# One weight slot per direction of a recurrence, and two projection tiles between its last links

## The reference, cut to what matters

```python
p = jnp.einsum('bsd,de->bse', h, w_in)
u, q, k, v, zr, gl = jnp.split(p, IN_SPLITS, axis=-1)
y_a = multiscale_pool(u, pool_w, pool_scale)
y_b = diff_attention(q, k, v, ...)
y_c = rwkv7_bidir(zr, ...)
```

```python
def step(state, inp):
    r_t, w_t, k_t, v_t, kk_t, a_t = inp
    sa = jnp.einsum('bhij,bhj->bhi', state, -kk_t)
    state = (state * w_t[:, :, None, :] + sa[..., None] * (kk_t * a_t)[:, :, None, :]
             + v_t[..., None] * k_t[:, :, None, :])
    return state, jnp.einsum('bhij,bhj->bhi', state, r_t)
...
y = direction(0, False) + direction(1, True)
mu = jnp.mean(y, axis=-1, keepdims=True)
var = jnp.mean(jnp.square(y - mu), axis=-1, keepdims=True)
y = ((y - mu) * lax.rsqrt(var + GN_EPS)).reshape(b, s, RW_WIDTH) * gn_g + gn_b
```

## Time and profile before

| | |
|---|---|
| median of 3 runs | 3981.09 us (3978.69 to 3983.14) |
| span of the profiled execution, first to last instruction | 3976.1 us |
| PE, busy | 3783.7 us (95%) |
| DVE, ACT, POOL, busy | 1684.3, 1439.1, 1388.7 us |
| transfers | 356.65 MB, 90 GB/s |
| mean granted TensorE clock | 0.984 |

### The profile page before, as it was taken

The page is one execution under the profiler, slowest core; times in us unless marked ns, Lnnn a source line. Parts: engine busy times, 40 slices in busy tenths (PEclk is TensorE's granted clock), DMA queues, the critical chain, the costliest instruction groups (busy, mean ns, idle before and its releaser), DMA issues.

```text
span 3976.1 us, 67100 instructions
## 1 busy us (share of the span) xinstructions
PE 3783.7 (95%) x28976; PEld 3059.2 (77%) x28976; DVE 1684.3 (42%) x2714; ACT 1439.1 (36%) x2442; POOL 1388.7 (35%) x581
## 2 busy tenths in 40 slices
PE   8888999999999889999999989999999999999999
PEld 7777778788887776688888776777888777787887
DVE  5554541577145554603682257414111376332112
ACT  3354252232323442523223243634222436424222
POOL 4001324434442002244444354133444443244443
PEclk9999999999999999999999999999999999999999
DMA  3001222276220002122473221112222221122222
GB/s 143 2 4 45 82 75 85 85 251 222 93 87 33 4 4 91 66 85 106 161 269 123 93 85 64 43 64 101 92 99 88 103 85 39 51 103 84 86 101 90
DMA packets 37150, 356.65 MB, mean 90 GB/s; under 512 B 4224, under 2 KB 4352, under 8 KB 17920
## 3 DMA queue, kind: packets, MB, share of 16 engines
q1 hardware_dynamic: 19584, 278.93, 18.9%
q10 hardware_dynamic: 17280, 73.48, 5.2%
HBM read 350.29 MB, written 2.10 MB: 89 GB/s over the span
## 4 chain that ended last, share of the span: by engine, by line
PE 84%; DVE 8%; ACT 3%; issue 2%; POOL 1%; DMA 1%; DVEq 0%; SPq 0%; PEldq 0%; ACTq 0%; PEld 0%; POOLq 0%
PE banks L757 23%; PE banks L759 23%; PE banks L758 22%; PE banks L1110 10%; PE banks L2151 3%; ACT arena L1471 1%; ACT arena L2304 1%; PE banks L2233 1%; POOL ring_r L855 1%; DMA ring<-stream 1%; DVE arena L1949 1%; DVE arena L2628 1%; PE banks L1217 0%; DVE arena L2627 0%; DVE arena L1843 0%
## 5 line engine op out<-in xcount | busy, mean ns | idle before, releaser
L855 POOL TENSOR_TENSOR ring_r<-ring,hi_ring 128x1024 fp32r<-128x1024 f32 x490 | 1202.4, 2458 | 2252.0 <-ACT hi_ring L846 2250.9
L757 PE MATMUL banks<-xT_r,ring_r 128*128 128x512 f32 (+1 forms) x2480 | 955.6, 385 | 25.8 <-issue 14.1
L759 PE MATMUL banks<-xT_r,hi_ring 128*128 128x512 f32 x2096 | 829.2, 396 | 0.0
L758 PE MATMUL banks<-x_lo_r,hi_ring 128*128 128x512 f32 x2096 | 825.4, 394 | 0.0
L846 ACT ACTIVATE hi_ring<-ring 128x1024 fp32r<-128x1024 f32 x490 | 511.3, 1047 | 734.0 <-DMA ring<-stream 289.2
L757 PEld LDWEIGHTS banks<-xT_r,ring_r 128*128 128x128 f32 x2480 | 472.5, 191 | 124.5 <-issue 26.7
L759 PEld LDWEIGHTS banks<-xT_r,hi_ring 128*128 128x128 f32 x2096 | 396.1, 189 | 94.1
L758 PEld LDWEIGHTS banks<-x_lo_r,hi_ring 128*128 128x128 f32 x2096 | 398.2, 190 | 90.3 <-issue 3.3
L1110 PE MATMUL banks<-arena 64*64 64x64 f32 (+4 forms) x7456 | 350.0, 246 | 53.0 <-DVE arena L1843 23.8
L1471 ACT ACTIVATE arena<-banks 128x512 f32<-128x512 f32 x366 | 214.7, 595 | 413.8 <-PE banks L759 255.2
L757 PE MATMUL banks<-hi_ring,pairs 128*128 128x512 f32 x864 | 341.8, 396 | 4.0 <-POOL ring_r L855 4.0
(11 more groups left out here) (263 smaller groups left out, 5504.1 us busy)
## 6 DMA issues: line engine op xcount, KB each, us to landing
ring<-stream SPq DMA_DIRECT2D x132, 2048.0 KB, 7.7
arena<-ada ACTq DMA_DIRECT2D x96, 512.0 KB, 4.9
arena<-ln_rows ACTq DMA_DIRECT2D x5, 1024.0 KB, 7.7
arena<-edge ACTq DMA_DIRECT2D x4, 1024.0 KB, 5.1
arena<-edge ACTq DMA_DIRECT2D x2, 1792.0 KB, 8.3
arena<-pack ACTq DMA_DIRECT2D x2, 1485.0 KB, 6.6
arena<-pack ACTq DMA_DIRECT2D x2, 1200.5 KB, 5.5
x<-x_in SPq DMA_DIRECT2D x4, 512.0 KB, 7.4
```

The lines of the kernel that those rows point to most:

```text
L757: first = nc.tensor.matmul(out_, left[1], right[0], start=start, stop=False)
L758: low = nc.tensor.matmul(out_, left[0], right[1], start=False, stop=False)
L759: return first, low, nc.tensor.matmul(out_, left[0], right[0], start=False, stop=stop)
L855: nc.gpsimd.tensor_tensor(feed.raw(n, ring_r), feed.raw(n), feed.hi(n).bitcast(F32), ALU.subtract).then_inc(split_lo, 1)
```

## The change

The matrices of a direction move into one slot each: direction 0 into the slot of unit 4, direction 1 into the slot of unit 5 (3072 columns of `GM`, 1024 of `WU`). Each slot is given back alone: behind link 6 of group 6 the one of direction 0, behind link 6 of group 7 the other (`slot_back`, a drain and one count each). `u`'s weights thus load while group 7 is computed. Its first tile is made in four parts of 6 products behind links 2, 3, 4 and 5 of group 7, the second in four, behind link 6, behind `y_out` (two) and behind the last mean. The pieces of `u` are split at `oo` of group 7, its links 1 and 5, and at the third part of the second tile; the third waits until group 6 is through, because its place in `hi_ring` holds that group's matrices. Three means go behind `mq`, `oo` and link 0 of group 7, the fourth behind `y_out`. The sums of squares go behind `u` 2, `gn_turn` behind `u` 3, and one `gn_out` behind each tile of `q`. Banks change with it.

```diff
--- before.py
+++ after.py
@@ -83,6 +83,8 @@
 EPS2 = 1e-6
 INDEX_SCALE = (64 ** -0.5) * (8 ** -0.5)
 UNITS1 = 35
+U_UNIT = 4
+U_PARTS = 2
 UNITS2 = 31
 X_LO = 27504
 W_HI = X_LO + 4096
@@ -173,8 +175,8 @@
                 ([] if last else [("inv_x", g, n, banks_x)]) + [("inv_t", g, n, banks_t)]]
     out += [[("wu", g, (b0, b1))], [("mq", g, (b0, b1))], [("oo", g, ())]]
     out += [[("link", g, i, (4 + i % 2,) if i < NC - 1 else ())] for i in range(NC)]
-    if g == GROUPS - 1:
-        out[-2].append(("ring_back", ()))
+    if g >= GROUPS - 2:
+        out[-2].append(("slot_back", d, ()))
     if d:
         out[-1].append(("y_out", j, (7,)))
     return out
@@ -248,22 +250,29 @@
         for n, beat in enumerate(beats_of(g)):
             if g or n >= AHEAD_BEATS:
                 late.setdefault(OFFSET * g + n - AHEAD_BEATS, []).append(beat)
+    end = GROUPS - 1
+    tail = {("mq", end): [("gn_mean", 0)], ("oo", end): [("gn_mean", 1)], ("link", end, 0): [("gn_mean", 2)],
+            ("link", end, 2): [("u_part", 0, 0)], ("link", end, 3): [("u_part", 0, 1)], ("link", end, 4): [("u_part", 0, 2)],
+            ("link", end, 5): [("u", 0)], ("link", end, 6): [("u_part", 1, 0)], ("y_out", PAIRS - 1): [("u_part", 1, 1)]}
+    tail_banks = {"gn_mean": (0, 1), "u_part": (), "u": (2, 3)}
     for n in sorted(late):
         for beat in late[n]:
             for part in beat:
                 add(*part[:-1], banks=part[-1])
-    for j in range(PAIRS):
-        add("gn_mean", j, banks=(j % 2,))
-    add("gn", banks=(0,))
-    behind = {("u", 1): [("gn_turn",)], ("u", 2): [("gn_out", 0)], ("u", 3): [("gn_out", 1)], ("q", 1): [("gn_out", 2)],
-              ("q", 3): [("gn_out", 3)],
+                for more_, i, *rest in tail.get(part[:-1], []):
+                    add(more_, i, *rest, banks=tail_banks[more_][i % 2:][:1])
+    add("u_part", 1, 2)
+    add("gn_mean", PAIRS - 1, banks=(1,))
+    add("u", 1, banks=(3,))
+    behind = {("u", 2): [("gn",)], ("u", 3): [("gn_turn",)], ("q", 0): [("gn_out", 0)], ("q", 1): [("gn_out", 1)],
+              ("q", 2): [("gn_out", 2)], ("q", 3): [("gn_out", 3)],
               ("k", 0): [("pool_mix", 0)], ("k", 1): [("pool_mix", 1), ("pool_lo", 0)],
               ("k", 2): [("pool_mix", 2), ("pool_lo", 1)], ("k", 3): [("pool_mix", 3), ("pool_lo", 2)]}
     for name in "uqk":
-        for i in range(4):
-            add(name, i, banks=(4 + i % 2,))
+        for i in range(U_PARTS if name == "u" else 0, 4):
+            add(name, i, banks=(2 + i % 2 if name == "u" else 4 + i % 2,))
             for late_, *at_ in behind.get((name, i), []):
-                add(late_, *at_, banks={"gn_turn": (1,), "gn_out": (0, 1, 2), "pool_mix": (sum(at_) % 2,)}.get(late_, ()))
+                add(late_, *at_, banks={"gn": (6,), "gn_turn": (6,), "gn_out": (0, 1, 6), "pool_mix": (sum(at_) % 2,)}.get(late_, ()))
     add("pool_lo", 3)
     add("v_open", banks=(2, 3, 4, 5))
     for i in range(4):
@@ -343,8 +352,9 @@
             add("next", ((2, 3, None, 7), (2, 4, 6, 9))[layer][tt])
     if layer == 0:
         add("turn", 1, 3, banks=(0, 4))
-    out = with_splits(out, first_pieces(), {ZT: ("u", 0), UP_PIECE + HEAD: ("turn", 0, 3)},
-                      {UP_PIECE + i: (("out_tile", 2), ("out_tile", 3))[i // 2] for i in range(HEAD)}, HEAD)
+    out = with_splits(out, first_pieces(), {ZT + 4: ("u", 2), UP_PIECE + HEAD: ("turn", 0, 3)},
+                      {**{UP_PIECE + i: (("out_tile", 2), ("out_tile", 3))[i // 2] for i in range(HEAD)},
+                       ZT: ("oo", end), ZT + 1: ("link", end, 1), ZT + 2: ("link", end, 5), ZT + 3: ("u_part", 1, 2)}, HEAD)
     return number(out)
 
 
@@ -436,7 +446,9 @@
 
 def first_pieces():
 
-    out = tile_pieces("z", 0, ZT) + tile_pieces("u", 4, 4) + tile_pieces("q", 5, 4) + tile_pieces("k", 6, 4) + row_pieces("v", 7)
+    out = tile_pieces("z", 0, ZT) + tile_pieces("u", U_UNIT, 4) + tile_pieces("q", 5, 4) + tile_pieces("k", 6, 4) + row_pieces("v", 7)
+    for i in range(U_PARTS):
+        out[ZT + i] = (("u_part", i, 0),) + out[ZT + i][1:]
     for n in range(3):
         out += tile_pieces("gate", 8 + 3 * n, DT, (n,)) + branch_pieces(n, 10 + 3 * n)
     out += row_pieces("out", 17, (0,)) + tile_row_pieces(18)
@@ -1009,8 +1021,14 @@
     BB = [arena[:, a_:a_ + 1024].rearrange("p (a t) -> p a t", a=2) for a_ in (17768, 18792)]
     X, XT, T1 = [[arena[:, a_ + 512 * d:a_ + 512 * d + 512].rearrange("p (b t) -> p b t", b=8) for d in range(2)]
                  for a_ in (19816, 20840, 21864)]
-    GM = [ring[:, 3072 * d:3072 * d + 3072].rearrange("p (q e b a t) -> p q e b a t", q=4, e=2, b=2, a=3) for d in range(2)]
-    WU = [ring[:, 6144 + 1024 * d:7168 + 1024 * d].rearrange("p (q e a t) -> p q e a t", q=4, e=2, a=2) for d in range(2)]
+    def in_slot(layer, d):
+
+        return UNIT * ((layer * UNITS1 + U_UNIT + d) % RING)
+
+    GM_of = [[ring[:, a_:a_ + 3072].rearrange("p (q e b a t) -> p q e b a t", q=4, e=2, b=2, a=3)
+              for a_ in (in_slot(layer, 0), in_slot(layer, 1))] for layer in range(L)]
+    WU_of = [[ring[:, a_ + 3072:a_ + UNIT].rearrange("p (q e a t) -> p q e a t", q=4, e=2, a=2)
+              for a_ in (in_slot(layer, 0), in_slot(layer, 1))] for layer in range(L)]
     AR0 = [arena[:, a_:a_ + 1024].rearrange("p (q e a t) -> p q e a t", q=4, e=2, a=2) for a_ in (22888, W_HI)]
     QM = [chunks(arena[:, a_:a_ + 1024], 2) for a_ in (W_HI + 1024, W_HI + 2048)]
     state = arena[:, 26984:27240].rearrange("p (d i k) -> p d i k", d=2, i=2)
@@ -1104,6 +1122,7 @@
 
     def first_tensor(pe, k_, layer, uses):
         feed = feed1[layer]
+        GM, WU = GM_of[layer], WU_of[layer]
         seen = {}
 
         def mm(out_, lhsT, rhs, start, stop):
@@ -1119,7 +1138,7 @@
                 return False
             seen[n] = True
             feed.wait_loaded(pe, n)
-            return n > 0 and n not in (3, 4)
+            return n > 0 and n not in (U_UNIT - 1, U_UNIT)
 
         def step(name, *args):
             banks, use = uses[(name,) + tuple(args)]
@@ -1134,6 +1153,14 @@
                     for turned in (0, 4):
                         pe.wait_ge(bank_free[turned], 2 - TT)
                 feed_product(pe, feed, feed.at["z", args[0]], bank[b][:, 0:S // 2], begin, x_pair, tokens=slice(0, S // 2))
+            elif name == "u_part" or name == "u" and args[0] < U_PARTS:
+                (b,), (n,) = uses[("u", args[0])]
+                part = args[1] if name == "u_part" else 3
+                if part == 0:
+                    take(b, n)
+                ins = feed_product(pe, feed, feed.at["u_part", args[0], 0], bank[b][:, :], begin, x_pair, part=part)
+                if part == 3:
+                    ins.then_inc(bank_full[b], 1)
             elif name in ("z", "u", "q", "k"):
                 i, b = args[0], banks[0]
                 head = name == "z" and i < HEAD
@@ -1327,9 +1354,9 @@
                              False, d == 1 and i == NC - 1)
                 if i == NC - 1:
                     ins.then_inc(*((bank_full[y_bank], 1) if d else (halves_done, 1)))
-            elif name == "ring_back":
-
-                pe.drain().then_inc(weights_used, RING)
+            elif name == "slot_back":
+
+                pe.drain().then_inc(weights_used, 1)
             elif name == "gn_mean":
                 j, b = args[0], banks[0]
                 take(b, use[0])
@@ -1647,6 +1675,8 @@
                     act.wait_ge(hid_lo, 0)
                 if name == "split" and args[0] == HEAD:
                     last_read(act)
+                if name == "split" and args[0] == ZT + 2:
+                    act.wait_ge(halves_done, halves(GROUPS - 1))
                 if name == "hid_split" and args[0] == 0:
                     act.wait_ge(mod_done, MODS)
                 feed_scalar(act, feed, name, args[0], uses, lambda m: act.wait_ge(hid_ready, m + 1))
@@ -1698,6 +1728,7 @@
 
     def first_vector(dve, k_, layer, uses, link):
         feed = feed1[layer]
+        GM = GM_of[layer]
         V = nc.vector
 
         def filled(b, n):
```

## The result

The kernel after takes 3992.41 us (12 runs, 3981.18 to 4003.30), the one before 3980.76 on the same chip (12 runs, 3974.57 to 3986.88): ratio 1.0032, 95% interval 1.0023 to 1.0042. It is 0.3% slower: 11.7 us between the medians, 12.7 by the ratio, where 4 us of gain were forecast.

What follows compares the result with a forecast made beforehand. TensorE, on the chain for 84% of the span, bounds the kernel; idle time and half clock at two seams were removable. Removed 17.3 us, new costs 13.8, gain 3.5 to 4: 3981.1 - 4.1 = 3977.0, range 3969 to 3983.

Steps and rivals of the forecast that it cites:

- one slot per direction, given back alone: Behind group 6's link 6: drain costs nothing, `u` loads early, 3.43 us stall goes; landing 5 us later costs nothing.
- the 3.43 us stall before `u`: Largest idle piece of TensorE between output products and `u`, behind drain, load, split and low part; forecast gone in both layers.
- Rival 2: `q`'s load is late, so ScalarE and TensorE wait before `u` 2's copy: up to 12 us slower, 3993; chance 7%.
- the edge of 9.1: Landing time of `q`'s load, in us, from which each further microsecond was to cost one, per layer.
- One sign of being wrong: ScalarE waiting for a DMA near 390; the other named sign was a clock of 1.0 through the norm.
- Rival 3: Links pay for the filling: splits and copies share ScalarE, switches cost 0.6, 3.6 us more, 3981; 14% together with rival 4.
- rival 4: The early load doesn't remove the stall because the DMA waits for something else: 3981; 14% together with Rival 3.
- Rival 1: Clock stays up through the norm or switches between product kinds are cheap: 3969 to 3972; chance 24%.
- The links: Links 2 to 5 of group 7 with parts of `u` between: cycle near 2.2 us, including 0.3 per turn.
- The norm's narrow products: Group norm's 16 products behind `u` 2: 1.4 us new waiting, then a clock fall costing 2.5 us, per layer.
- 0.453 us lost for each at half rate: Prediction's price of half clock, from `u`'s product spacing 0.235 against 0.43 us; 6.12 us low in layer 1 cost 2.8.
- The sum without the failed step: Forecast gain split by layer: about 1.3 us in layer 0 and about 2.4 in layer 1.

Runs made afterwards that it cites:

- e12: e8 with direction 0's slot back behind `wu` of group 7 and 512 KB tiles asked for there, at links 0, 3, 5: 3968.45 us, ratio 0.9973 against before.
- e1: Kernel before with only one slot per direction and the early give-back, so `u`'s 2 MB load early: 3990.99 us, ratio 1.0038.
- e2: Kernel before with only an added drain behind link 6 of group 6, no load there: 3977.63 us, ratio 1.0006.
- e6: e1 with direction 0's slot given back later, behind `oo` of group 7: 3975.4 us, ratio 0.9994 against the kernel before.
- e10: Kernel before with a useless 2 MB HBM-to-HBM transfer per layer behind link 6 of group 3: 3989.7 us, ratio 1.0035.
- e5: e1 with 1 MB of `u`'s load at the early give-back, 1 MB at the late one: 3993.87 us, ratio 1.0043 against before.
- e8: Changed kernel, `u` loaded in 512 KB tiles, squares ahead, narrow products in four groups among `u` 2's parts: 3972.84 us, ratio 0.9992 against before.

## Why the prediction was wrong

**The step that failed** is the first of "Part by part", *one slot per direction, given back alone*. Its other terms are right one by one: the drain is hidden, the load starts at 355.17 (forecast 355.9) and takes 9.0 us (forecast 7.67), well inside its slack of 5 us, ScalarE doesn't wait for it, and the 3.43 us stall before `u` is gone in both layers. What fails is the price of nothing for the transfer itself. It was weighed against SyncE's queue and ScalarE's work only; that instructions come by DMA too stood on the profile's page as queue 8, 232 packets, and was not asked after. The term that was missing, by the two traces: 4.05 + 3.6 = 7.7 us of pause and, of work at half the clock behind it, 2.9 + about 1.8 in layer 0 (`mq` took 1.98 instead of 1.10 us, the first mean likewise) and 1.2 in layer 1. That is 13.6 us, beside the 16 to 17 between the forecast's gain of 4 and the measured loss of 12 to 13. The rest isn't located, since the profiled execution is the fastest of its kernel. By the mean clocks (0.983 over the twelve runs, 0.985 in the kernel before) an ordinary run of it has some 16 us more half clock, which is 7 us by an estimate that takes TensorE as busy all the while. Of a step that is moved, not only the transfer it issues counts, but the transfers that this one meets.

**Rival 2**, the slower one, had the right sign with another mechanism. `q`'s load is asked for at 391.81 and lands 9.07 later, on the edge of 9.1 from which it was to cost; the wait in front of the narrow products is 1.30 us in both layers, which is the forecast's, so lateness of `q` cost next to nothing. One sign of being wrong that the prediction named did come, though: ScalarE waits for this transfer, 3.05 us until 400.90 and 2.74 us in layer 1. It is through just in time for the copy of `u` 2, and in layer 0 the chain of waits runs over it: had it landed later, it would have cost.

**Rival 3** (the links pay for the filling) and **rival 4** (the stall stays) didn't come. **Rival 1** (the clock stays up, 3972) didn't come in the kernel after, but e12 shows that it can be had: with the narrow products in fours between full ones, and no lengthened pause, the clock stays at 1.00 through both seams and the time is 3968.45.

**What held.**
- *The links.* With a part of `u` in them, a cycle is 2.2 us: parts start at 381.35, 383.57, 385.78 and 388.00 in the kernel after. Forecast "near 2.2", with 0.3 for a turn of kind. The Trainium skill says that a weight load can be pulled ahead of running products ("TensorE: Matmul & The Clock Gate", "Step-by-step: what each phase is for"); that doesn't make these turns free here.
- *The norm's narrow products* wait 1.30 us (forecast 1.4), and the clock falls while they run, without a long pause before: 6.8 us low in layer 0, 3.4 in layer 1, at the prediction's 0.453 us lost for each at half rate 3.1 and 1.5 against the forecast's 2.5. The Trainium skill's rule on long idle gaps (the same page, "HAM oscillation") doesn't foretell this fall. It does foretell the one at the 5 us pause: 13.7 us low in layer 0, though only 3.4 in layer 1 at a like pause.
- *The sum without the failed step*: in layer 1 the way from `mq` to the last output became 3.0 us shorter, forecast 2.4. In layer 0 it became 1.4 longer, of which 1.8 is the half clock from the pause: 0.4 better, forecast 1.3. (The prediction's own terms give 17.3 - 13.8 = 3.5 us of gain; the forecast took 4.1, 0.6 more than they add up to.)

**What stays inferred.** That the packets of queue 8 missing from 351.4 to 360.5 are TensorE's is read from the pause that ends 2.5 us behind the next one; the profile doesn't say which engine a packet feeds. That the transfer brings the pause is shown (e1, e2, e6, e10, e12); by which path it does isn't, and something else that a transfer and TensorE share isn't excluded. Why a pause is followed by a long half clock in one layer and by a short one in the other is open; after, e1 and e5 have 3.4 to 34 us of it behind pauses of 3.9 to 5.1. The half-clock time of a whole trace goes from 91 us (e8) to 167 (e5), and a part of each ratio above is that.

## What to carry to other kernels

A transfer that nobody waits for isn't free when it is moved: before it is started earlier, look at what TensorE does while it runs (8 to 9 us for 2 MB here), and keep large loads out of stretches of many short instructions. An "issue" pause that already stands in the profile is a hint at such a place, but not a condition: the place of e10 had none. Put them beside few, long instructions, or cut them so that a piece is asked for where it fits. And narrow products, here, kept the clock up in small groups between full ones.

## What the runs showed of the hardware that was not expected

- A 2 MB load beside small products stops TensorE for 4.6 to 5.1 us instead of 1.0 to 1.4; a transfer from HBM to HBM of 2 MB does so too, 3.1 and 3.3 us, where there was no pause.
- The pause isn't proportional to the bytes: 512 KB make 2.35 and 3.02, 1 MB 4.00 and 3.91, 2 MB 4.55 and 4.73. Paced in four, 2 MB make only 2.35 and 1.86.
- The same 16 narrow products bring the clock down in one run of 16 (0.66 over 404 to 414) and not in four runs of four (1.00 over 391 to 403 in e12), where the wait of 1.30 us before them is gone too.
